# A one-core decoder layer: half-wise first unit, float32r conditioning sums, tiled forget gate, half-wise last scatter

## The chip, the cores and the metric

The kernel runs on one core of one Trainium2 chip. The metric is the device time of one launch, in microseconds. Before the change it was 780.5 us, the median of three runs (780.03 to 780.75).

## What is computed

One layer of a decoder trunk over x (1, 256, 1024), in float32, conditioned by one vector c (cut to what matters):

```python
mod = silu(c) @ W_ada + b_ada            # 6 x 1024: shift/scale/gate of the mixer and of the FFN
h = rms_norm(x) * (1 + scale_m) + shift_m
proj = h @ w_in                          # pool, sg_u, sg_v, conv_a, conv_g, q, k, v, f_logit (4), gates (4 x 1024)
y_a = multiscale_pool(z_pool);  y_b = spatial_gating(z_sg)
y_c = silu(layer_norm(causal_conv31(a * sigmoid(g))))
y_d = forgetting_attention(q, k, v, f_logit + b_f)   # softmax(qk + cum log_sigmoid(f))
merged = sum_n sigmoid(gates_n) * (y_n @ w_branch_n)
x = x + gate_m * (merged @ w_out)
h = rms_norm(x) * (1 + scale_f) + shift_f
x = x + gate_f * (moe(h) + shared(h))    # 64 experts, 6 per token, 1024 -> 256 -> 1024
return rms_norm(x)
```

## The kernel before, in words

Every engine's work stands in program order in one block per engine, and semaphores alone tie the blocks together. There is no planner: what an engine does next is what is written next.

**Weights.** SyncE (SP) streams all weights through a ring of 12 slots of 1 MB (L361: dense units in the order of `UNITS`; L364 and L369: experts). A load into a slot waits until the unit that was in it is used up. The last 16 `ada` units are used up by VectorE (`acc_done`), the others by TensorE. For the experts the ring holds two pairs; the loads of pair n+2 wait for TensorE's use of pair n (`w13_used`, `w2_used`).

**Start.** TensorE multiplies eight `ada` units with the conditioning vector (`ada(0)` to `ada(7)`, four column tiles of 32), and `columns(i)` turns the sums into columns. VectorE makes the scale a_c and shift s_c, and ScalarE (L478) and VectorE (L697) write the eight k-slices of hT, four after `columns(1)` and four after `columns(3)`, each counted by `h_done`.

**Mixer units.** `channels(i, u)` (L1166) runs 16 float32 products of 128x256; each is two MATMUL records. Units `mix 0` to `mix 7` are conv_g, conv_a, q, k, v, sg_v, sg_u and pool. All of them start after `h_done >= 8` (L1194). The forget logits are eight products with 4 columns of weights each, between units 2 and 3. VectorE adds the bias (L711) and, with ScalarE, makes log-sigmoid and its running sum; ScalarE then starts two small DMAs (L508, L509) that put the sums into the rows `qa[64]` and `ka[65]`, and the attention's logits on TensorE wait for them (`cum_rows`, L1206).

**Gate loop.** For g = 0 to 15 TensorE runs `channels(8 + g)` and then `branch(g - 3)` (LAG = 3) (L1275). At g = 3 it sums the convolution's channels, at g = 4 the squares (`cvar_done`). ScalarE takes one sigmoid per g (L557); at g = 4 it also does the layer norm's square root (L560) and the swish's sigmoid (L562). VectorE's order is: `conv_norm_1`, `accumulate(0)`, `conv_norm_2`, `accumulate(1)`, normalise and swish to `y[:, 2]` (L887 to L891), and then per g: `merge(g)`, at odd g from 3 on `cast_out`, `accumulate(g + 2)`. `accumulate(i)` adds four slices of a late `ada` unit, scaled, into `part2` (L753); two of them make one sum of 512 columns, and `cast(m)` on TensorE (L1250) adds that over the partitions by one float32 product with a matrix of ones, 128x512. Casts 0 to 5 run at g = 5, 7, ..., 15, `cast(6)` after the last branch.

**Out stage.** Four groups of eight 128x512 products with w_out, then `cast(7)` (L1324). VectorE does `accumulate(14)` and `accumulate(15)` before the first residual (`residual_2(0)`, L909).

**Experts.** Routing, then 32 pairs of experts; per pair the w1/w3 products, a gather for the next group, the scatter of the pair before, and the w2 products. VectorE splits each result into two float32r parts (L1076), counted by `y_split`; the scatter (L1392) waits for both halves. After the last pair the final scatter and norm follow.

Of the kernel before, what the change touches and what calls it, by code (L numbers as in the profile page):

```python
# [69 lines left out]
def unit_plan():  # L70
    units = [("ada", i) for i in range(8)] + [("mix", i) for i in range(8)]
    for g in range(N_GATE):
        if g % 4 == 3:
# [15 lines left out]
         "fold": 64, "inv": 512, "iota": CAP, "thr": 3, "mask": 384}  # L89
# [13 lines left out]
MISC = {"wf": KD * HEADS, "sg_w": HEADS * P, "pool_w": 2 * P, "sg_g": BW, "sg_beta": BW, "sg_bias": 2 * T}  # L103
# [7 lines left out]
def decoder_layer(nc, a, out):  # L111
    with ExitStack() as ctx:
# [50 lines left out]
        wf = mi("wf", "p (k h) -> p k h", h=HEADS)  # L163
# [26 lines left out]
        with ExitStack() as mixing:  # L190
            def early(name, shape):
                return mixing.enter_context(nc.sbuf_tensor(name, shape, F32))
# [24 lines left out]
            sig = c6(LAG + 2, 2 * T)  # L217
            gb = c6(2 * T)
            logit = sig[:, 0:2, 0:384]
            v_sb = sig[:, 2, :].rearrange("p (b c) -> p b c", b=TB)  # L220
# [9 lines left out]
            rden = early("rden", [P, HEADS, 2])  # L230
            fz = sig[0:HEADS, 3:5, :].rearrange("p a t -> p (a t)")[:, 0:3 * T].rearrange("p (r t) -> p r t", r=3)
# [16 lines left out]
        def gathered_row(parity, k):  # L248
# [21 lines left out]
        B_CAST = [3, 3, 3, 3, 3, 3, 3, 2]  # L270
# [15 lines left out]
            unit_done f_done f_read exp_f cum_done cum_rows  conv_done  # L286
# [4 lines left out]
            gb_done merged_done branch_done acc_done cast_done cast_read out_mm  # L291
# [3 lines left out]
            sw2_gated x2_top give_read y0_done y_gated y_top y_split pos_next sum_done x3_sq x3_var x3_rstd fin_done stored""".split()  # L295
# [162 lines left out]
        def _(act):  # L458
# [25 lines left out]
            def ub(i):  # L484
# [3 lines left out]
            act.activation(sig_c[:, :, :].rearrange("p j t -> p (j t)"), ub(0)[:, :], ACT.Sigmoid)\  # L488
               .then_inc(unit_read[0], 1)
            read_unit(2)  # L490
            act.wait_ge(S["zero_done"], 6)
# [59 lines left out]

            for g in range(N_GATE):

                read_unit(8 + g)
                if g >= LAG + 2:
                    act.wait_ge(S["gb_done"], g - LAG - 1)
                act.activation(sig[:, g % (LAG + 2), :], ub(g)[:, :], ACT.Sigmoid).then_inc(unit_read[g % 2], 1)  # L557
                if g == CONV_AT:
                    act.wait_ge(S["conv_var"], 1)
                    act.activation(mean_c[:, :], rs_c[:, :], ACT.Sqrt).then_inc(S["conv_rstd"], 1)  # L560
                    act.wait_ge(S["conv_n"], 2)
                    act.activation(sq_c[:, :, :], conv[:, :, :], ACT.Sigmoid).then_inc(S["conv_sig"], 1)  # L562
# [30 lines left out]

            square_2(0)
            square_2(1)
# [74 lines left out]
        def _(dve):  # L670
# [33 lines left out]
            dve.wait_ge(S["unit_done"], 2)  # L704
            dve.wait_ge(unit_read[0], 1)
# [5 lines left out]
            dve.tensor_scalar(fz[:, 0, :], bank[7][0:HEADS, 0:T], par[0:HEADS, P_AT["b_f"]:P_AT["b_f"] + 1], None,  # L711
# [155 lines left out]
            def cast_out(m):  # L867
# [3 lines left out]
                dve.wait_ge(S["cast_done"], m + 1)  # L871
# [7 lines left out]
                ins.then_inc(S["cast_read"], 1)  # L879

# [47 lines left out]
            residual_2(0)  # L928
            residual_2(1)
# [114 lines left out]
            def body(use):  # L1044
                for m in range(BODY_PAIRS):
# [21 lines left out]
                    for hf in range(2):  # L1067
                        if hf:
                            dve.wait_ge(w2_used[r], use * (BODY_PAIRS // 2) + m // 2 + 1)
                        else:  # L1070
# [6 lines left out]
                           .then_inc(S["y_split"], 1)  # L1077
# [38 lines left out]
        def _(pe):  # L1116
# [36 lines left out]
            ada(5)  # L1153
            ada(6)
            columns(2)
# [10 lines left out]
            def channels(i, u):  # L1166

                b, w = begin_unit(i, u)
                for m in range(2):
                    for k in range(KD):  # L1170
                        ins = mm(b[:, m * T:(m + 1) * T], w[:, k, m * P:(m + 1) * P], hT[:, k, :], k == 0, k == KD - 1)
                ins.then_inc(S["unit_done"], 1)
# [21 lines left out]
            pe.wait_ge(S["h_done"], 8)  # L1194
            channels(0, ("mix", 0))
# [79 lines left out]
            for g in range(N_GATE):  # L1275
# [13 lines left out]
                if g % 2 and g >= 5:  # L1289
                    cast((g - 5) // 2)  # L1290
# [4 lines left out]
            cast(6)  # L1295
# [28 lines left out]
            cast(7)  # L1324

# [75 lines left out]
            def body(use):  # L1401
                for m in range(BODY_PAIRS):
# [19 lines left out]
                    if not first:  # L1422
                        pe.wait_ge(S["y_split"], 2 * n)
# [9 lines left out]
                    if not first:  # L1433
                        scatter(1 - r, 0, opening)
                        scatter(1 - r, 1, opening)
# [43 lines left out]
            last = passes * (2 * PAIRS)  # L1479
            pe.wait_ge(S["give_read"], passes * PAIRS)  # L1480
            pe.wait_ge(S["y_split"], last)
            for hf in range(2):
                scatter(1, hf, stop=True).then_inc(S["sum_done"], 1)


def constants():
# [14 lines left out]
    c["iota"][:] = np.arange(CAP)  # L1501
    c["fold"][:] = i % E == np.arange(E)
# [4 lines left out]
def lay_out(inp):  # L1507
# [9 lines left out]
    wf = inp["w_in"][0][:, COL["f"]:COL["f"] + HEADS].reshape(KD, P, HEADS).transpose(1, 0, 2).reshape(P, KD * HEADS)  # L1517
# [35 lines left out]
```

## Time and profile before

| | |
|---|---|
| median of three runs | 780.5 us |
| the profiled execution | 781.12 us |
| its span, first to last instruction | 779.3 us |
| mean granted TensorE clock | 0.989 |
| PE busy | 730.0 us (94%) |
| PE weight loads | 387.9 us (50%) |
| DVE busy | 326.3 us (42%) |
| ACT busy | 172.2 us (22%) |
| HBM traffic | 271.33 MB, mean 348 GB/s |

PE is TensorE's matmuls, PEld its weight loads, DVE VectorE, ACT ScalarE, SPq the queue of SyncE. A busy share is an average over stages with different limits, so it doesn't say what a change in one stage is worth; the waits and the chain that ended last do.

### The profile page before, as it was taken

Reading aid. Unit: us, or ns where it says so; the run is one execution under the profiler, and the core shown is the slowest. Engines: PE = TensorE matmul, PEld = TensorE weight load, DVE = VectorE, ACT = ScalarE, POOL = GpSimd, SP = SyncE. Lnnn points to the kernel's source line nnn. Section 1 sums busy time; section 2 is a strip of 40 time slices with the busy share of each in tenths; the row PEclk is TensorE's granted clock in tenths of the full one; section 3 lists DMA queues with packets and bytes.
Section 4 is the critical chain, followed back from the end, with each engine's and each line's share of the span. In section 5 each row is a group of like instructions: output and inputs, shape, how many; then the busy total and the mean of one; then the engine's idle time right before and its main releaser. Section 6 shows DMA issues by size and latency. Waiting matters only on the chain.

```text
span 779.3 us, 12407 instructions
## 1 busy us (share of the span) xinstructions
PE 730.0 (94%) x5000; PEld 387.9 (50%) x5000; DVE 326.3 (42%) x814; ACT 172.2 (22%) x344; POOL 8.7 (1%) x22
## 2 busy tenths in 40 slices
PE   4799999999999999999999999999999999899894
PEld 1388888888887444334333343333334333333232
DVE  1107675674446577333334233231333333323325
ACT  3213240200000241222222122121222222212213
POOL 0200001000000000000000000000000000000000
PEclk9799999999999999999999999999999999999998
DMA  9999535777869676999999999999999999999981
GB/s 339 378 349 365 190 108 189 237 260 259 264 221 385 262 274 240 392 422 421 421 417 420 419 420 421 421 421 408 409 420 422 420 419 422 421 421 420 421 353 55
DMA packets 73571, 271.33 MB, mean 348 GB/s; under 512 B 4440, under 2 KB 33248, under 8 KB 48688
## 3 DMA queue, kind: packets, MB, share of 16 engines
q1 hardware_dynamic: 71808, 264.26, 86.3%
q0 software_dynamic: 1408, 6.20, 2.1%
q8 instruction: 40, 0.66, 0.3%
q10 hardware_dynamic: 304, 0.13, 0.1%
q14 instruction: 11, 0.09, 0.0%
HBM read 269.51 MB, written 1.05 MB: 347 GB/s over the span
## 4 chain that ended last, share of the span: by engine, by line
PE 67%; DMA 21%; DVE 6%; SPq 3%; ACT 2%; issue 1%; DVEq 0%; ACTq 0%
PE bank L1118 65%; DMA ring<-exp_w_dram 19%; DMA ring<-ada_w_dram 2%; SPq L364 1%; DVE slot_gate L1054 1%; SPq L361 1%; PE bank L1438 1%; DVE reg L1058 1%; DVE reg L1049 1%; ACT reg L632 1%; DMA reg<-reg 1%; DVE h_hT L1109 0%; PE bank L1138 0%; DVE stats L1096 0%; DVE bank L1072 0%
## 5 line engine op out<-in xcount | busy, mean ns | idle before, releaser
L1118 PE MATMUL bank<-ring,h_hT 128*32 128x512 f32 (+2 forms) x2112 | 255.4, 586 | 14.3 <-DMA ring<-exp_w_dram 13.5
L1118 PEld LDWEIGHTS bank<-ring,h_hT 128*32 128x32 f32 (+1 forms) x2112 | 84.6, 113 | 170.8 <-issue 151.2
L1118 PE MATMUL bank<-h_hT,ring 128*128 128x256 f32 x704 | 158.4, 385 | 1.8 <-ACT h_hT L478 1.8
L1118 PEld LDWEIGHTS bank<-h_hT,ring 128*128 128x128 f32 x704 | 135.5, 193 | 21.4 <-ACT h_hT L478 2.0
L1118 PE MATMUL bank<-ring,const_misc 128*32 128x512 f32 x1008 | 116.5, 595 | 0.3
L1049 DVE TENSOR_TENSOR reg<-reg,bank 128x256 f32<-128x256 f32 x32 | 13.5, 421 | 180.7 <-ACT reg L632 180.7
L1072 DVE TENSOR_TENSOR bank<-bank,reg 128x512 f32<-128x512 f32 x64 | 44.5, 695 | 54.6 <-PE bank L1118 54.6
L1076 DVE TENSOR_TENSOR y_part<-bank,y_part 128x512 fp32r<-128x512 f32 x64 | 44.3, 692 | 42.4 <-ACT y_part L645 21.2
L1118 PEld LDWEIGHTS bank<-ring,const_misc 128*32 128x32 f32 x1008 | 30.2, 109 | 61.6 <-issue 57.3
L632 ACT ACTIVATE reg<-bank 128x256 f32<-128x256 f32 x32 | 12.3, 384 | 198.8 <-PE bank L1118 198.8
L1118 PE MATMUL bank<-take,h_part 128*128 128x256 f32 x288 | 50.6, 299 | 0.4 <-ACT h_hT L617 0.2
L753 DVE SCALAR_TENSOR_TENSOR part<-ring,cact,part 128x512 f32<-128x512 f32 x56 | 42.0, 749 | 1.9 <-DVE part L753 0.2
L1118 PE MATMUL bank<-y_part,give 64*128 64x512 f32 x256 | 38.5, 418 | 2.4 <-DVE y_part L1076 2.4
L1118 PEld LDWEIGHTS bank<-take,h_part 128*128 128x128 f32 x288 | 38.8, 190 | 1.9 <-ACT h_hT L617 1.0
L627 ACT ACTIVATE h_hT<-bank 128x512 f32<-128x512 f32 x64 | 38.1, 595 | 3.8 <-PE bank L1118 0.3
L557 ACT ACTIVATE reg<-bank 128x512 f32<-128x512 f32 x16 | 9.6, 597 | 113.9 <-PE bank L1118 112.5
L643 ACT ACTIVATE y_part<-bank 128x512 fp32r<-128x512 f32 x32 | 19.1, 597 | 66.8 <-DVE bank L1072 66.8
L1118 PE MATMUL bank<-reg,ring 128*128 128x256 f32 x128 | 29.7, 379 | 0.0
L645 ACT ACTIVATE y_part<-bank 128x512 fp32r<-128x512 f32 x32 | 19.1, 597 | 43.6 <-DVE bank L1072 43.6
L862 DVE TENSOR_TENSOR reg<-bank,reg 128x512 f32<-128x512 f32 x16 | 11.1, 691 | 40.8 <-PE bank L1118 39.9
L1118 PE MATMUL bank<-ring,reg 128*128 128x512 f32 x64 | 27.8, 592 | 0.0
L1118 PEld LDWEIGHTS bank<-reg,ring 128*128 128x128 f32 x128 | 24.3, 190 | 5.9 <-issue 2.8
(231 smaller groups left out, 450.5 us busy)
## 6 DMA issues: line engine op xcount, KB each, us to landing
ring<-exp_w_dram SPq DMA_DIRECT2D x189, 1024.0 KB, 14.9
ring<-ada_w_dram SPq DMA_DIRECT2D x24, 1024.0 KB, 12.5
ring<-w_in_dram SPq DMA_DIRECT2D x24, 1024.0 KB, 12.3
ring<-w_branch_dram SPq DMA_DIRECT2D x4, 1024.0 KB, 12.9
ring<-w_out_dram SPq DMA_DIRECT2D x4, 1024.0 KB, 8.0
ring<-shared_w_dram SPq DMA_DIRECT2D x2, 1024.0 KB, 13.8
spare<-exp_w_dram SPq DMA_DIRECT2D x2, 1024.0 KB, 16.2
reg<-ada_bp_dram POOLq DMA_DIRECT2D x3, 512.0 KB, 8.3
```

What stands on the lines that cost most here:

```text
L361: sp.dma_start(dst, src).then_inc(landed[SLOT[u]], 16)
L557: act.activation(sig[:, g % (LAG + 2), :], ub(g)[:, :], ACT.Sigmoid).then_inc(unit_read[g % 2], 1)
L627: act.activation(gathered_row(1 - m // GROUP, 2 * (m % GROUP) + q), bank[B_GATH][:, :].rearrange("p (m s) -> p m s", m=GROUP), ACT.Copy)\
L632: act.activation(sg1[:, :], bank[B_HID][:, 0:FF], ACT.Sigmoid).then_inc(S["sig1_done"], 1)
L643: act.activation(y_part[0][:, 0:512], bank[B_Y[0]][:, :], ACT.Copy).then_inc(S["y_top"], 1)
L645: act.activation(y_part[0][:, 512:D], bank[B_Y[1]][:, :], ACT.Copy).then_inc(S["y_top"], 1)
L753: ins = dve.scalar_tensor_tensor(out=acc, in0=w[:, q, :], scalar=at, in1=acc, op0=ALU.mult, op1=ALU.add)
L862: dve.tensor_tensor(o, bank[4 + g % 2][:, :], sig[:, g % (LAG + 2), :], ALU.mult).then_inc(S["gb_done"], 1)
L1049: dve.tensor_tensor(th[:, :], sg1[:, :], bank[B_HID][:, 0:FF], ALU.mult).then_inc(S["th_done"], 1)
L1072: dve.tensor_tensor(bank[B_Y[hf]][:, :], bank[B_Y[hf]][:, :], gate_f[:, hf * 512:(hf + 1) * 512], ALU.mult)\
L1076: dve.tensor_tensor(y_part[1][:, cols], bank[B_Y[hf]][:, :], y_part[0][:, cols], ALU.subtract)\
L1118: return pe.matmul(o, lhsT, rhs, start=start, stop=stop, skip_group_check=True)
```

## The change

- The first mixer unit runs in two halves of k: its two outputs go to two banks (0 and 4), the first half of each after `h_done >= 4`, the second after `h_done >= 8`. `columns(2)` is moved ahead of `ada(6)`.
- The forget logits are computed in four column tiles of 32 (weights padded from 4 to 32 columns), copied out by ScalarE, and folded by one more product in the middle of unit 3.
- Each conditioning sum is cast in halves of 256 columns. ScalarE copies the half as float32r (`cast_top`), VectorE makes the rest (`cast_rest`), and TensorE adds two float32r products. There are 16 such casts; cast c stands ahead of `branch(c + 1)` at g = c + 4 for c = 0 to 11, the next two among the last branches, the last two behind the first and the second group of the out stage.
- `y_split` becomes `y_low` and `y_high`, and each half of the scatter waits for its own.

```diff
@@ ScalarE
             read_unit(0)
-            act.activation(sig_c[:, :, :]..., ub(0)[:, :], ACT.Sigmoid).then_inc(unit_read[0], 1)
+            act.activation(sig_c[:, 0, :], bank[B_UNIT_0[0]][:, 0:T], ACT.Sigmoid).then_inc(S["g_top"], 1)
+            act.activation(sig_c[:, 1, :], bank[B_UNIT_0[1]][:, 0:T], ACT.Sigmoid).then_inc(unit_read[0], 1)
             read_unit(2)
+            act.wait_ge(S["f_half"], 1)
+            act.activation(f_tiles[:, :], bank[7][:, 0:T], ACT.Copy).then_inc(S["f_tiled"], 1)
...
+            def cast_top(c):
+                act.wait_ge(S["acc_done"], 2 * (c // 2) + 2)
+                if c:
+                    act.wait_ge(S["cast_done"], c)
+                act.activation(cast_part[:, 0, :], part2[:, c // 2 % 2, (c % 2) * 256:(c % 2 + 1) * 256], ACT.Copy)\
+                   .then_inc(S["cast_top"], 1)
             for g in range(N_GATE):
...
+                if g >= LAG:
+                    cast_top(g - LAG)
...
+            cast_top(N_GATE - 3)
+            cast_top(N_GATE - 2)
             square_2(0)
+            cast_top(N_GATE - 1)
             square_2(1)
@@ VectorE
+            link(dve.tensor_copy(ones_r[:, :], cn("ones", 0, P)))
...
                 if half == 0 and m >= 2:
-                    dve.wait_ge(S["cast_done"], m - 1)
+                    dve.wait_ge(S["cast_rest"], 2 * (m - 1))
...
+            def cast_rest(c):
+                dve.wait_ge(S["cast_top"], c + 1)
+                dve.tensor_tensor(cast_part[:, 1, :], part2[:, c // 2 % 2, ...], cast_part[:, 0, :],
+                                  ALU.subtract).then_inc(S["cast_rest"], 1)
...
             for g in range(N_GATE):
                 merge(g)
+                if g not in (N_GATE - 3, N_GATE - 1):
+                    cast_rest(min(g, N_GATE - 3))
                 if g % 2 and g >= 3:
                     cast_out((g - 3) // 2)
                 if g + AHEAD < N_GATE - 2:
                     accumulate(g + AHEAD)
             accumulate(N_GATE - 2)
             accumulate(N_GATE - 1)
+            cast_rest(N_GATE - 2)
...
             residual_2(0)
+            cast_rest(N_GATE - 1)
             residual_2(1)
@@ TensorE
             ada(5)
+            columns(2)
             ada(6)
-            columns(2)
             ada(7)
             columns(3)
...
-            pe.wait_ge(S["h_done"], 8)
-            channels(0, ("mix", 0))
+            pe.wait_ge(S["h_done"], KD // 2)
+            w = begin_unit(0, ("mix", 0))[1]
+            for half in range(2):
+                if half:
+                    pe.wait_ge(S["h_done"], KD)
+                for m in range(2):
+                    for k in range(half * (KD // 2), (half + 1) * (KD // 2)):
+                        ins = mm(bank[B_UNIT_0[m]][:, 0:T], w[:, k, m * P:(m + 1) * P], hT[:, k, :], k == 0, k == KD - 1)
...
             for k in range(KD):
-                ins = mm(bank[7][0:HEADS, 0:T], wf[:, k, :], hT[:, k, :], k == 0, k == KD - 1)
-            ins.then_inc(S["f_done"], 1)
-            channels(3, ("mix", 3))
+                ins = mm(bank[7][32 * (k % 4):32 * (k % 4) + 32, 0:T], wf[:, k, :], hT[:, k, :], k < 4, k >= 4)
+            ins.then_inc(S["f_half"], 1)
+            channels(3, ("mix", 3), forget_sum)
...
-            def cast(m):
-                pe.wait_ge(S["acc_done"], 2 * m + 2)
-                if m:
-                    pe.wait_ge(S["cast_read"], min(m, 6))
-                mm(bank[B_CAST[m]][:, :], cn("ones", 0, P), part2[:, m % 2, :]).then_inc(S["cast_done"], 1)
+            def cast(c):
+                m, half = c // 2, c % 2
+                pe.wait_ge(S["cast_rest"], c + 1)
+                if m >= 2 and not half:
+                    pe.wait_ge(S["cast_read"], m - 1)
+                for i in range(2):
+                    ins = mm(bank[B_CAST[m]][:, half * 256:(half + 1) * 256], ones_r[:, :], cast_part[:, i, :], i == 0, i == 1)
+                ins.then_inc(S["cast_done"], 1)
...
-                if g % 2 and g >= 5:
-                    cast((g - 5) // 2)
+                if g > LAG:
+                    cast(g - LAG - 1)
                 if g >= LAG:
                     branch(g - LAG)
             for g in range(N_GATE - LAG, N_GATE):
                 branch(g)
-            cast(6)
+                if g != N_GATE - 2:
+                    cast([N_GATE - 4, None, N_GATE - 3][g - (N_GATE - LAG)])
...
-            cast(7)
+                if k < 2:
+                    cast(N_GATE - 2 + k)
...
-            pe.wait_ge(S["y_split"], last)
             for hf in range(2):
+                pe.wait_ge(S["y_high" if hf else "y_low"], last)
                 scatter(1, hf, stop=True).then_inc(S["sum_done"], 1)
```

`forget_sum` waits for `f_tiled` and runs one product `mm(bank[7][0:HEADS, T:2 * T], cn("fold_f"), f_tiles)`, which counts `f_done`; `channels` calls it between its two outputs.

## Rows read from the trace of the kernel before

**Rows 1.** Page, part 2: GB/s in 40 slices of the span.
```profile
GB/s 339 378 349 365 190 108 189 237 260 259 264 221 385 262 274 240 392 422 421 421 417 420 419 420 421 421 421 408 409 420 422 420 419 422 421 421 420 421 353 55
```
**Rows 2.** Chain that ended last: start us, us, what.
```profile
99.24 170.53 PE bank L1118 x754
...
463.91 19.16 DMA ring<-exp_w_dram
```
**Rows 3.** Timeline of SP's queue: start us, us, engine line, operation.
```profile
311.42 2.04 SPq L364 DMA_DIRECT2D ring<-exp_w_dram  x4
```
**Rows 4.** Timeline, start to first unit; in brackets idle before and its releaser.
```profile
28.14 0.20 PEld L1118 LDWEIGHTS bank<-ring,crep 128*32 128x32 f32 x8 [0.33 <-DMA ring<-ada_w_dram]
...
32.42 24.00 PE L1118 MATMUL bank<-h_hT,ring 128*128 128x256 f32 x96 [1.77 <-ACT h_hT L478]
```
**Rows 5.** First unit's load: issue (timeline), then its size and us to landing.
```profile
14.45 4.63 SPq L361 DMA_DIRECT2D ring<-w_in_dram  x1
...
ring<-w_in_dram SPq DMA_DIRECT2D x1, 1024.0 KB, 16.5
```
**Rows 6.** Windows: PE, PEld, DVE, ACT, POOL busy (x), PEclk, DMA share, GB/s.
```profile
25.00:28.00 3.00, 2.77 (x12) 0.92 (x12) 0.00 (x0) 0.00 (x0) 0.00 (x0) 0.50 1.06 377
...
33.00:38.00 5.00, 5.00 (x13) 4.01 (x12) 0.00 (x0) 0.66 (x1) 1.61 (x2) 0.50 1.06 396
```
**Rows 7.** Timeline of the forget logits, table load and rows; chain's line of their DMA.
```profile
56.34 3.62 PE L1118 MATMUL bank<-h_hT,const_misc 128*4 128x256 f32 x16
61.39 1.28 ACT L500 ACT_TABLE_LOAD   x1
62.68 0.41 ACT L500 ACTIVATE reg<-reg 4x256 f32<-4x256 f32 x1
64.29 0.28 DVE L722 TENSOR_SCALAR reg<-reg 4x256 f32<-4x256 f32 x1
...
68.36 5.84 DMA reg<-reg
...
74.34 2.86 PE L1118 MATMUL bank<-reg 66*128 66x128 f32 x16 [0.37 <-DMA reg<-reg]
```
**Rows 8.** Timeline: one cast, the out stage behind it; a gather and a scatter.
```profile
248.15 1.02 PE L1118 MATMUL bank<-part,const_misc 128*128 128x512 f32 x2
...
249.01 20.76 PE L1118 MATMUL bank<-ring,reg 128*128 128x512 f32 x48
...
324.95 0.68 PE L1118 MATMUL bank<-take,h_part 128*128 128x256 f32 x4
325.56 1.21 PE L1118 MATMUL bank<-y_part,give 64*128 64x512 f32 x8
```
**Rows 9.** Timeline around g = 4 of the gate loop, all engines.
```profile
140.46 0.60 ACT L557 ACTIVATE reg<-bank 128x512 f32<-128x512 f32 x1 [8.90 <-PE bank L1118]
...
141.13 1.89 PE L1118 MATMUL bank<-reg,ring 128*128 128x256 f32 x8
...
143.46 3.02 DVE L753 SCALAR_TENSOR_TENSOR part<-ring,cact,part 128x512 f32<-128x512 f32 x4
143.57 0.42 ACT L560 ACTIVATE reg<-reg 128x256 f32<-128x256 f32 x1 [1.21 <-DVE reg L851]
...
148.32 0.63 ACT L562 ACTIVATE reg<-reg 128x512 f32<-128x512 f32 x1 [3.03 <-DVE reg L888]
...
149.59 0.69 DVE L862 TENSOR_TENSOR reg<-bank,reg 128x512 f32<-128x512 f32 x1
```
**Rows 10.** Page, part 5: work on 256 columns; busy, mean ns, idle before.
```profile
L1049 DVE TENSOR_TENSOR reg<-reg,bank 128x256 f32<-128x256 f32 x32 | 13.5, 421 | 180.7 <-ACT reg L632 180.7
...
L632 ACT ACTIVATE reg<-bank 128x256 f32<-128x256 f32 x32 | 12.3, 384 | 198.8 <-PE bank L1118 198.8
```
**Rows 11.** Timeline: VectorE at the end of `accumulate(15)`, and in the tail.
```profile
253.43 3.12 DVE L753 SCALAR_TENSOR_TENSOR part<-ring,cact,part 128x512 f32<-128x512 f32 x4 [0.23 <-DVE part L753]
...
771.46 1.43 DVE L1096 BATCH_NORM_STATS2 stats<-bank 128x6 f32<-128x512 f32 x2 [0.90 <-PE bank L1118]
```

More of the change, by code:

```diff
@@ L88 @@
 CONST = {"ident": 128, "upper": 128, "strict": 128, "ones": 256,
-         "fold": 64, "inv": 512, "iota": CAP, "thr": 3, "mask": 384}
+         "fold": 64, "fold_f": HEADS, "inv": 512, "iota": CAP, "thr": 3, "mask": 384}
 C_AT, C_W = {}, 0
@@ L101 @@
     P_W += _w
-MISC = {"wf": KD * HEADS, "sg_w": HEADS * P, "pool_w": 2 * P, "sg_g": BW, "sg_beta": BW, "sg_bias": 2 * T}
+MISC = {"wf": KD * 32, "sg_w": HEADS * P, "pool_w": 2 * P, "sg_g": BW, "sg_beta": BW, "sg_bias": 2 * T}
 M_AT, M_W = {}, 0
@@ L161, in mi @@
             return misc[:, M_AT[name]:M_AT[name] + MISC[name]].rearrange(pattern, **kw)
-        wf = mi("wf", "p (k h) -> p k h", h=HEADS)
+        wf = mi("wf", "p (k h) -> p k h", h=32)
         sgw = mi("sg_w", "p (h t) -> p h t", h=HEADS)
@@ L190, in decoder_layer, with early @@
         with ExitStack() as mixing:
-            def early(name, shape):
-                return mixing.enter_context(nc.sbuf_tensor(name, shape, F32))
+            def early(name, shape, dt=F32):
+                return mixing.enter_context(nc.sbuf_tensor(name, shape, dt))
             reg1 = early("reg1", [P, 2 * D])
@@ L219, in decoder_layer @@
             logit = sig[:, 0:2, 0:384]
+            f_tiles = sig[:, 0, 0:T]
             v_sb = sig[:, 2, :].rearrange("p (b c) -> p b c", b=TB)
@@ L230, in decoder_layer @@
             rden = early("rden", [P, HEADS, 2])
+            ones_r = early("ones_r", [P, P], F32R)
+            cast_part = early("cast_part", [P, 2, 256], F32R)
             fz = sig[0:HEADS, 3:5, :].rearrange("p a t -> p (a t)")[:, 0:3 * T].rearrange("p (r t) -> p r t", r=3)
@@ L269, in decoder_layer @@
         B_UNIT = [0, 1]
-        B_CAST = [3, 3, 3, 3, 3, 3, 3, 2]
+        B_UNIT_0 = [0, 4]
+        B_CAST = [3, 2, 3, 2, 3, 2, 3, 2]
         B_OUT = [0, 1, 2, 3]
@@ L285, in decoder_layer @@
             final_in c_sig c_rep x_sq x_var x_rstd xn_done xT_done ada_done ada_read col_done acc_step ac_done h_done
-            unit_done f_done f_read exp_f cum_done cum_rows  conv_done
+            unit_done g_top f_half f_tiled f_done f_read exp_f cum_done cum_rows  conv_done
             q_done k_done tv_done sigv_done v_var v_rstd vn_done tu_done sigu_done
@@ L290, in decoder_layer @@
             logits_done logit_done exp_done prob_done pT_done pT_read av_done av_y
-            gb_done merged_done branch_done acc_done cast_done cast_read out_mm
+            gb_done merged_done branch_done acc_done cast_top cast_rest cast_done cast_read out_mm
             x2_done x2_sq x2_var x2_rstd h2_done h2T_done h2T_read
@@ L294, in decoder_layer @@
             take_built pair_gates gate_mm slot_gated gathered gath_read first_read sig1_done th_done hid_done turn_done turn_read
-            sw2_gated x2_top give_read y0_done y_gated y_top y_split pos_next sum_done x3_sq x3_var x3_rstd fin_done stored""".split()
+            sw2_gated x2_top give_read y0_done y_gated y_top y_low y_high pos_next sum_done x3_sq x3_var x3_rstd fin_done stored""".split()
         S = {n: sem(n) for n in names}
@@ L702, in _ @@
                 dve.tensor_tensor(sgw[:, h, :], sgw[:, h, :], cn("upper"), ALU.mult).then_inc(S["sgw_done"], 1)
+            link(dve.tensor_copy(ones_r[:, :], cn("ones", 0, P)))
             dve.wait_ge(S["unit_done"], 2)
+            dve.wait_ge(S["g_top"], 1)
             dve.wait_ge(unit_read[0], 1)
@@ L710, in _ @@
             dve.wait_ge(S["f_done"], 1)
-            dve.tensor_scalar(fz[:, 0, :], bank[7][0:HEADS, 0:T], par[0:HEADS, P_AT["b_f"]:P_AT["b_f"] + 1], None,
+            dve.tensor_scalar(fz[:, 0, :], bank[7][0:HEADS, T:2 * T], par[0:HEADS, P_AT["b_f"]:P_AT["b_f"] + 1], None,
                               ALU.add).then_inc(S["f_read"], 1)
@@ L870, in cast_out @@
                 dst = [gate_m, scale_b, shift_f, gate_f][m // 2][:, cols]
-                dve.wait_ge(S["cast_done"], m + 1)
+                dve.wait_ge(S["cast_done"], 2 * m + 2)
                 if m == 0:
@@ L879, in cast_out @@
                 ins.then_inc(S["cast_read"], 1)
+            def cast_rest(c):
+                dve.wait_ge(S["cast_top"], c + 1)
+                dve.tensor_tensor(cast_part[:, 1, :], part2[:, c // 2 % 2, (c % 2) * 256:(c % 2 + 1) * 256], cast_part[:, 0, :],
+                                  ALU.subtract).then_inc(S["cast_rest"], 1)
             conv_norm_1()
@@ L1076, in body @@
                         dve.tensor_tensor(y_part[1][:, cols], bank[B_Y[hf]][:, :], y_part[0][:, cols], ALU.subtract)\
-                           .then_inc(S["y_split"], 1)
+                           .then_inc(S["y_high" if hf else "y_low"], 1)
             with dve.Fori(0, 1) as use:
@@ L1164, in begin_unit, with forget_sum, channels @@
                 return bank[B_UNIT[i % 2]], unit(u).rearrange("p (k n) -> p k n", k=KD)
-            def channels(i, u):
+            def forget_sum():
+                pe.wait_ge(S["f_tiled"], 1)
+                mm(bank[7][0:HEADS, T:2 * T], cn("fold_f"), f_tiles[:, :]).then_inc(S["f_done"], 1)
+            def channels(i, u, between=None):
                 b, w = begin_unit(i, u)
                 for m in range(2):
+                    if m and between:
+                        between()
                     for k in range(KD):
@@ L1192, in turn_probs @@
                 ins.then_inc(S["pT_done"], 1)
-            pe.wait_ge(S["h_done"], 8)
-            channels(0, ("mix", 0))
+            pe.wait_ge(S["h_done"], KD // 2)
[6 more added lines that the diff above has]
+                        ins = mm(bank[B_UNIT_0[m]][:, 0:T], w[:, k, m * P:(m + 1) * P], hT[:, k, :], k == 0, k == KD - 1)
+            ins.then_inc(S["unit_done"], 1)
             channels(1, ("mix", 1))
@@ L1422, in body @@
                     if not first:
-                        pe.wait_ge(S["y_split"], 2 * n)
+                        pe.wait_ge(S["y_low"], n)
                     pe.wait_ge(S["pair_gates"], n + 1)
@@ L1434, in body @@
                         scatter(1 - r, 0, opening)
+                        pe.wait_ge(S["y_high"], n)
                         scatter(1 - r, 1, opening)
@@ L1478, in _ @@
                 body(use)
-            last = passes * (2 * PAIRS)
-            pe.wait_ge(S["give_read"], passes * PAIRS)
-            pe.wait_ge(S["y_split"], last)
+            last = passes * PAIRS
+            pe.wait_ge(S["give_read"], last)
             for hf in range(2):
+                pe.wait_ge(S["y_high" if hf else "y_low"], last)
                 scatter(1, hf, stop=True).then_inc(S["sum_done"], 1)
@@ L1501, in constants @@
     c["iota"][:] = np.arange(CAP)
+    c["fold_f"][:] = i % 32 == np.arange(HEADS)
     c["fold"][:] = i % E == np.arange(E)
@@ L1516, in lay_out @@
     par = np.concatenate(cols + [b_f], 1)
-    wf = inp["w_in"][0][:, COL["f"]:COL["f"] + HEADS].reshape(KD, P, HEADS).transpose(1, 0, 2).reshape(P, KD * HEADS)
+    wf = inp["w_in"][0][:, COL["f"]:COL["f"] + HEADS].reshape(KD, P, HEADS).transpose(1, 0, 2)
+    wf = np.pad(wf, ((0, 0), (0, 0), (0, 32 - HEADS))).reshape(P, KD * 32)
     sg_w = inp["sg_w"][0].transpose(2, 0, 1).reshape(P, HEADS * P)
```

2 lines of the change are left out of this document (removed).

## The prediction, made before the changed kernel ran

> **What bounds the kernel now.** I read the page's slices first. From about 312 us to 755 us the DMA moves some 420 GB/s in almost every slice [rows 1], so the experts go at the pace of their weights. Before that it moves 108 to 392 GB/s and something else is the limit. The chain of waits says what: from 99.24 to 269.77 us it is nothing but TensorE, and late in the expert stage it runs over the expert loads [rows 2]. Last I looked at the queue that issues the loads, to see what starts the saturated stream. Pair 2 of the experts is issued at 311.42 us [rows 3], as soon as TensorE has used pair 0's w1 and w3. From there the stream is full, so what is left after 311.42 us is bytes by 420 GB/s and a tail. Every microsecond that TensorE gains or loses before 311 us therefore shifts the end by the same amount; the sum below is one of TensorE's path up to there, and of the tail.
>
> **First unit in halves.** The four early slices of hT are ready before TensorE gets there (it still has `ada` units and `columns(3)` to do, written ahead of the unit). Now it waits 1.77 us for the last four slices and starts at 32.42 us [rows 4]. After the change it can start when `columns(3)` is out, at 30.65 us (32.42 - 1.77), unless the unit's weights are late: issued at 14.45 us, 16.5 us to land [rows 5], so 30.95 us. The start is 1.47 us earlier. Moving `columns(2)` ahead of `ada(6)` buys nothing: `ada(7)` already waits for its load [rows 4], and what was behind it now fills an idle gap. To the start comes the clock. It was granted at half (1.2 of 2.4 GHz) both from 25 to 28 us and from 33 to 38 us [rows 6]; in the second the first units lost 2.9 us: their 96 records took 24.0 us, where six times the 3.5 us of sixteen such records [rows 7] is 21.1. With less idle time in front of it I take a low stretch as short as the first one, which loses some 1.6 us instead of 2.9: another 1.3. Term: **-2.8**; with no low stretch -4.4, and if the earlier start is worth only half because the clock is low as long as before, -0.8.
>
> **Forget gate.** Sixteen records take 3.62 us, 3.55 us of TensorE's time [rows 7]. In four column tiles they should take a quarter, 0.9 us plus about 0.15 for filling, and the fold one 128x256 float32 product, 0.44 us. TensorE saves 2.1 us. But the logits behind wait for the two rows that the small DMA writes: they landed 0.37 us after TensorE was ready [rows 7]. That DMA needs unit 3 (now earlier by 2.1 us) and the running sum, which was ready 64.57 - 59.96 = 4.6 us after the logits. The logits now come 5.1 us after unit 2 (1.05, half of unit 3, the fold), the sum at 9.7, and the second DMA's issue near 10.4, with 5.84 us to landing [rows 7] 16.3 us, against 18.0 us now (56.34 to 74.34). Term: **-1.7** (-2.1 if the DMA is quicker, -1.2 if slower). ScalarE's extra copy (0.38 us) stands ahead of the q copies, which nobody waits for within 10 us; later VectorE work keeps 4 us or more of slack.
>
> **Casts as work.** A 128x512 float32 cast takes 0.86 us (248.15 to 249.01 [rows 8]). Four float32r products of 128x256 take 0.61 us until the next group starts (324.95 to 325.56 [rows 8]), 0.153 each, so a cast of 256 columns takes 0.31 us. Six casts leave the gate loop, thirteen come in up to the last branch: 13 x 0.31 - 6 x 0.86 = **-1.1**. The rows bound it from 0.2 us (the scatter's eight products, 1.21 us with their fill, handle twice the columns [rows 8]) to 0.5 us each: -2.6 to +1.3.
> The Trainium skill (TensorE: Matmul & The Clock Gate, Back-to-back issue gap) gives 262 cycles between products of 256 columns. By that rule a cast would take about 0.22 us, and the forecast would be 1.2 us lower; the gather in this trace is slower than that, and I go by the row.
>
> **The first cast as a wait.** This is the large term. Before, no cast stood at g = 4; now `cast(0)` does, in front of `branch(1)`, which started at 141.13 us [rows 9]. It waits for `cast_rest(0)`, and that stands on VectorE behind the whole layer norm of the convolution, which itself starts only from `cvar_done`, TensorE's instruction just before. And ScalarE now has `cast_top(0)` at g = 3, waiting for `accumulate(1)`; queued behind it are the sigmoid of g = 4 and the square root that the layer norm needs. In the times of before: `accumulate(1)` ends at 146.5 us (143.46 + 3.02 [rows 9]). Then ScalarE: copy 0.40 (384 ns [rows 10]), sigmoid 0.60, table load 1.30 (1.28 us, formerly hidden behind the wait for VectorE [rows 7, 9]), root 0.42 [rows 9]: 149.4. VectorE's four normalising steps took 1.7 us (146.6 to 148.32, where the swish started); now 151.1. Swish 0.63, product 0.61, so the first merge, 149.59 us before [rows 9], starts at 152.4, ends at 153.0, and `cast_rest(0)` (421 ns [rows 10]) at 153.4. TensorE stands still from 141.13 to 153.43: **+12.3** (11.8 to 12.8 by what the handovers add or save). Nothing hides it: `branch(1)` and the next unit, which filled that time, are now written behind the cast, and this engine runs its matmuls in the order in which they are written. Behind it the ring is full and VectorE catches up, since per unit it needs 0.42 (rest), 1.4 (merge), 0.7 to 1.4 (cast_out) and 3.1 us of TensorE's 9 (a unit's 7.1 and a branch's 1.9); so `cast(1)` and later ones should find their halves ready.
> The Trainium skill (ScalarE: Activation LUTs, What ACT_TABLE_LOAD costs) puts 1283 ns for the load and 1380 ns of drain on every switch of table. By that rule the exposed load would make the stall 1.4 us longer; in this trace an activation starts 0.01 us after a load ends (61.39 + 1.28 to 62.68 [rows 7]), so I count 1.30.
>
> **The clock after it.** TensorE has never idled for 12 us in the trace; after much shorter gaps in the first 40 us the clock was at half [rows 6]. So it should restart at 1.2 GHz. The two low stretches there cost 1.5 us (3 us at half) and 2.9 us: **+2.3** (1.5 to 3.1).
>
> **Out stage.** From the last branch (248.15 us): `cast(13)` 0.31, first group 20.76 / 3 = 6.9 us [rows 8], so TensorE reaches `cast(14)` at +7.2. VectorE first does both last accumulates, which ended at 256.55 us = +8.4 [rows 11]; then copy 0.40, rest 0.42 and handovers [rows 10]: +9.35. The stall is 2.15 us. `cast(14)` and `cast(15)` add 0.62, `cast(13)` 0.31, `cast(6)` leaves with 0.86; `cast(13)` is in the thirteen above, which leaves out the removed `cast(6)`, so the stage's own sum is 2.15 + 0.62 - 0.86 + 0.3 of rounding and fill: **+2.25** (1.5 to 2.9). The removed `cast(7)` gives nothing: VectorE's last residual ran beside it. After a 2.15 us gap the clock may fall too: 0 or 1.7 us, I take **+0.8**.
>
> **Tail.** The scatter of half 0 moves ahead, under the split of half 1. VectorE idled 0.90 us before two statistics steps of 1.43 us [rows 11]; the first now fills that gap: **-0.7** (0 to -0.9). Elsewhere in the expert stage the two waits change nothing, as weights are the limit.
>
> **Sum.** -2.8 - 1.7 - 1.1 + 12.3 + 2.3 + 2.25 + 0.8 - 0.7 = +11.4. The profiled execution took 781.1 us (span 779.3), so 792.5 for it; it is 0.6 us above the median of the runs, and the forecast for the median is 780.5 + 11.4 = **791.9 us**.
>
> **Rivals.**
> *Ready halves (other side, 5%).* The halves of `cast(0)` are made before TensorE gets there. Then +12.3 and +2.3 fall away: 777.3 us. The point that decides is whether `cast_rest(0)` ends before 141.13 us in the times of before. For it: the accumulates' data are there early. Against it: the first merge ran at 149.59 us [rows 9] and the rest is written behind it.
> *ScalarE not in the way (8%).* The root comes as early as before. The stall is then merge at 149.59 plus 1.05, 9.5 us: 789.1 us. Against it: the root is written behind `cast_top(0)`.
> *Hidden by the experts (4%).* The dense stage's loss is absorbed, because loads run ahead during the stall. Then only the tail moves: 779.8 us, no change. Against it: pair 2's load waits for TensorE [rows 3], and the ring holds two pairs only.
> *Every cast stalls (5%).* VectorE never catches up, and each of eleven later casts waits a microsecond: 803 us. Against it: the budget of about 6 of 9 us.
> The forecast has 78%.
>
> **Range and chances.** The terms' bounds added at their worst give 785 and 800 us; they are not all at one end, so 785.5 to 797 us, which takes in the second rival. About 0.2% (1.6 us) is what a measurement of this kernel can tell from no change. Faster 6%, same 4%, slower 90%.
>
> **What would show it.** An idle gap of some 12 us on TensorE before `cast(0)`, ended by VectorE's rest; ScalarE's sigmoid of g = 4 behind `accumulate(1)`; the granted clock at 0.5 just after; a gap near 2 us before `cast(14)`; unit 0 starting near 31 us; pair 2's load some 12 us later than 311.42, and the same 420 GB/s behind it. I am wrong if the gap is absent or the shift at pair 2 doesn't reach the end.

## The result

The changed kernel takes 791.1 us, the median of four runs (790.18 to 792.42), against 780.6 us for the kernel before (780.03 to 781.6): ratio 1.0133, 95% interval 1.0118 to 1.0148. It is 10.5 us slower. Its profiled execution took 792.4 us, with a span of 790.6 us against 779.3.

### The profile page after: what moved, and what is told of

It is laid out like the page before. It is cut to its first block, busy times and chain, and to the rows that moved or that the text cites. A ratio compares the mean times of both kernels' runs of the same rounds, so it can differ in the third digit from the quotient of the medians.

```text
span 790.6 us, 12494 instructions
## 1 busy us (share of the span) xinstructions
PE 725.0 (92%) x5018; PEld 387.5 (49%) x5018; DVE 331.8 (42%) x831; ACT 177.8 (22%) x362; POOL 8.7 (1%) x22
## 4 chain that ended last, share of the span: by engine, by line
PE 63%; DMA 21%; DVE 8%; SPq 3%; ACT 2%; issue 2%; DVEq 0%; ACTq 0%
PE bank L1150 62%; DMA ring<-exp_w_dram 18%; DMA ring<-w_in_dram 2%; SPq L365 2%; SPq L368 1%; DVE slot_gate L1086 1%; PE bank L1488 1%; DVE reg L1090 1%; DVE part L775 1%; DVE reg L1081 1%; ACT reg L652 1%; DMA reg<-reg 1%; DVE reg L884 0%; DVE h_hT L1141 0%; DVE reg L887 0%
## 5 line engine op out<-in xcount | busy, mean ns | idle before, releaser
L652 ACT ACTIVATE reg<-bank 128x256 f32<-128x256 f32 x32 | 12.3, 384 | 200.3 <-PE bank L1150 200.3
L571 ACT ACTIVATE reg<-bank 128x512 f32<-128x512 f32 x16 | 9.5, 596 | 108.3 <-PE bank L1150 108.3
L1150 PEld LDWEIGHTS bank<-y_part,give 64*128 64x128 f32 x256 | 21.6, 184 | 9.9 <-DVE y_part L1108 1.6
## 6 DMA issues: line engine op xcount, KB each, us to landing
ring<-ada_w_dram SPq DMA_DIRECT2D x24, 1024.0 KB, 12.8
ring<-w_branch_dram SPq DMA_DIRECT2D x4, 1024.0 KB, 12.8
```

The source lines that it names most:

```text
L652: act.activation(sg1[:, :], bank[B_HID][:, 0:FF], ACT.Sigmoid).then_inc(S["sig1_done"], 1)
L1150: return pe.matmul(o, lhsT, rhs, start=start, stop=stop, skip_group_check=True)
```

## The profile after

The page of the changed kernel first: total busy time and the slices. PE's busy time fell by 5 us and its share from 94% to 92%; the rate of the experts' stage is the same 420 GB/s, but it starts about half a slice later: slice 17 has 298 GB/s where it had 392 [rows 1].

```profile
span 790.6 us, 12494 instructions
PE 725.0 (92%) x5018; PEld 387.5 (49%) x5018; DVE 331.8 (42%) x831; ACT 177.8 (22%) x362; POOL 8.7 (1%) x22
GB/s 339 379 348 364 199 81 235 217 76 367 177 337 271 368 145 332 298 412 419 421 420 420 421 422 421 420 421 421 377 419 422 421 418 422 422 419 421 423 368 54
```

Next the chain that ended last, the rows that answer to the one long piece of TensorE [rows 2]; they are from the list of its longest pieces, so short ones between them are left out. It is now broken between 138 and 150 us and once more before 265.90:

```profile
96.05 42.07 PE bank L1150 x220
138.64 1.63 issue
144.30 1.28 ACT L574
150.07 102.31 PE bank L1150 x478
265.90 14.47 PE bank L1150 x36
```

The timeline of the changed kernel around g = 4, all engines, answers to [rows 9]. TensorE ends the sum of squares at 138 us and does nothing until VectorE's `cast_rest(0)` (L906) is out; cuts between the lines are marked. ScalarE's first float32r copy (L563) waited 15.00 us for `accumulate(1)`, and only behind it come the sigmoid of g = 4 (L571), the table load and the root (L574):

```profile
137.08 1.03 PE L1150 MATMUL bank<-reg,const_misc 128*128 128x256 f32 x4
...
140.27 3.02 DVE L775 SCALAR_TENSOR_TENSOR part<-ring,cact,part 128x512 f32<-128x512 f32 x4
...
143.38 0.42 ACT L563 ACTIVATE cast_part<-part 128x256 fp32r<-128x256 f32 x1 [15.00 <-DVEq L780]
143.70 0.58 ACT L571 ACTIVATE reg<-bank 128x512 f32<-128x512 f32 x1
...
144.30 1.28 ACT L574 ACT_TABLE_LOAD   x1
145.59 0.42 ACT L574 ACTIVATE reg<-reg 128x256 f32<-128x256 f32 x1
...
147.73 0.63 ACT L576 ACTIVATE reg<-reg 128x512 f32<-128x512 f32 x1 [0.42 <-DVE reg L916]
...
149.00 0.68 DVE L884 TENSOR_TENSOR reg<-bank,reg 128x512 f32<-128x512 f32 x1
149.60 0.41 DVE L906 TENSOR_TENSOR cast_part<-part,cast_part 128x256 fp32r<-128x256 f32 x1
...
150.07 0.80 PE L1150 MATMUL bank<-cast_part,ones_r 128*128 128x256 f32 x2 [11.96 <-DVE cast_part L906]
...
150.66 3.05 PE L1150 MATMUL bank<-reg,ring 128*128 128x256 f32 x8
```

L576 is the swish, which before ran at 148.32 us (L562). The same `branch(1)` took 1.89 us before and 3.05 us here. The windows of the changed kernel (busy per engine, granted clock third from the right) say why: the clock fell to half during the idle time and was back at full in the window from 153 us.

```profile
138.00:141.00 3.00, 0.11 (x1) 0.00 (x0) 2.79 (x4) 0.00 (x0) 0.00 (x0) 1.00 1.03 374
141.00:144.00 3.00, 0.00 (x0) 0.00 (x0) 2.22 (x3) 0.62 (x2) 0.00 (x0) 0.79 0.11 43
...
147.00:150.00 3.00, 0.00 (x0) 0.00 (x0) 2.27 (x6) 0.94 (x2) 0.00 (x0) 0.50 1.05 341
150.00:153.00 3.00, 2.93 (x8) 2.48 (x9) 2.67 (x5) 0.42 (x1) 0.00 (x0) 0.50 0.32 110
153.00:156.00 3.00, 3.00 (x15) 2.64 (x15) 1.79 (x4) 0.00 (x0) 0.00 (x0) 1.00 0.67 183
```

TensorE in the changed kernel at the places of [rows 4, 7, 8]: the first unit, the forget logits in tiles, their fold, the attention's logits, a cast in the loop with its branch, and the cast in the out stage that waits.

```profile
31.01 14.18 PE L1150 MATMUL bank<-h_hT,ring 128*128 128x256 f32 x51 [0.58 <-DMA ring<-w_in_dram]
...
54.83 1.07 PE L1150 MATMUL bank<-h_hT,const_misc 128*32 128x256 f32 x16
...
59.48 0.59 PE L1150 MATMUL bank<-reg,const_misc 128*4 128x256 f32 x2
...
71.16 2.86 PE L1150 MATMUL bank<-reg 66*128 66x128 f32 x16 [0.52 <-DMA reg<-reg]
...
160.27 0.59 PE L1150 MATMUL bank<-cast_part,ones_r 128*128 128x256 f32 x2
...
162.42 7.07 PE L1150 MATMUL bank<-h_hT,ring 128*128 128x256 f32 x32
169.14 0.58 PE L1150 MATMUL bank<-cast_part,ones_r 128*128 128x256 f32 x2
169.56 1.89 PE L1150 MATMUL bank<-reg,ring 128*128 128x256 f32 x8
171.29 7.07 PE L1150 MATMUL bank<-h_hT,ring 128*128 128x256 f32 x32
...
265.90 0.50 PE L1150 MATMUL bank<-cast_part,ones_r 128*128 128x256 f32 x2 [1.63 <-DVE cast_part L906]
```

Pair 2's load in the changed kernel, which answers to [rows 3]: 10.6 us later than 311.42.

```profile
322.03 2.25 SPq L368 DMA_DIRECT2D ring<-exp_w_dram  x4
```

The tail of the changed kernel: the scatter is split in two, and the first statistics step (L1128) has no wait in front any more [rows 11].

```profile
780.78 0.73 PE L1150 MATMUL bank<-y_part,give 64*128 64x512 f32 x4 [0.55 <-DVE y_part L1108]
...
782.51 0.69 DVE L1128 BATCH_NORM_STATS2 stats<-bank 128x6 f32<-128x512 f32 x1
...
782.65 0.73 PE L1150 MATMUL bank<-y_part,give 64*128 64x512 f32 x4 [1.14 <-DVE y_part L1108]
...
783.50 0.70 DVE L1128 BATCH_NORM_STATS2 stats<-bank 128x6 f32<-128x512 f32 x1 [0.29 <-PE bank L1150]
```

## The experiments

All times are medians, beside the kernel before on the same chip (780.96 us for e1 to e4, 780.77 us for e5 to e8, spread 777.7 to 782.8). The ratios are not the quotients of the medians: 775.99 to 780.96 is 0.9936 where the ratio of e3 is 0.9941, so a difference of medians can be half a microsecond or more off what the ratio says.

The traces allow a comparison that leaves the start of the kernel, and its clock, out: the distance from the attention's logits on TensorE to pair 2's load.

| | attention's logits | pair 2's load | distance, us |
|---|---|---|---|
| before | 74.34 | 311.42 | 237.08 |
| changed | 71.16 | 322.03 | 250.87 |
| e1_late_cast | 71.09 | 309.25 | 238.16 |
| e2_scalar_order | 71.00 | 320.27 | 249.27 |
| e3_old_casts | 68.71 | 305.79 | 237.08 |
| e4_unit_twice | 74.31 | 318.27 | 243.96 |
| e5_late_both | 68.27 | 304.42 | 236.15 |
| e6_products_twice | 70.88 | 310.33 | 239.45 |
| e7_no_halves | 71.31 | 308.40 | 237.09 |
| e8_old_casts_again | 68.19 | 305.27 | 237.08 |

**e1_late_cast.** Every cast of the gate loop one unit later, and behind the branch instead of ahead of it: `cast(0)` goes from before `branch(1)` to behind `branch(2)`. `cast(13)`, `cast(14)` and `cast(15)` stay where they were. ScalarE's `cast_top` and VectorE's `cast_rest` move along.

```diff
 # ScalarE                                   # VectorE
-if g >= LAG: cast_top(g - LAG)             -if g not in (13, 15): cast_rest(min(g, 13))
+if g > LAG: cast_top(g - LAG - 1)          +if g not in (1, 15): cast_rest(max(g - 1, 0))
 # TensorE
-if g > LAG: cast(g - LAG - 1)
 if g >= LAG: branch(g - LAG)
+if g > LAG + 1: cast(g - LAG - 2)
...
-if g != N_GATE - 2: cast([N_GATE - 4, None, N_GATE - 3][g - (N_GATE - LAG)])   # last three branches
+cast(g - 2)
```

> The changed kernel with its casts one unit later: cast(c) stands behind branch(c + 2) at g = c + 5, cast_top(c) one unit later on ScalarE, cast_rest(c) one merge later on VectorE (only rest 0 stays behind the first merge). Theory (the first cast's wait is the loss): the stall of 12.1 us before cast(0) goes, and with it 1.3 us at half clock; 10.6 us above before becomes about 2.8 below, 777.5 us. Rival (the casts as such cost TensorE or VectorE more than they save, wherever they stand): less than 6 us of the loss comes back, 785 us or more. Rival (the delay was not what reached the end): no change from 791 us.

Measured: 778.3 us (ratio to before 0.9962, 0.9946 to 0.9978). The kernel is 12.8 us faster than the change as written. TensorE of e1 at the same place: its only stop there is half a microsecond for the first merge, and `cast(0)` stands behind `branch(2)` without a wait.

```profile
137.88 1.89 PE L1151 MATMUL bank<-reg,ring 128*128 128x256 f32 x8
139.60 7.07 PE L1151 MATMUL bank<-h_hT,ring 128*128 128x256 f32 x32
147.17 1.97 PE L1151 MATMUL bank<-reg,ring 128*128 128x256 f32 x8 [0.50 <-DVE reg L885]
148.79 0.59 PE L1151 MATMUL bank<-cast_part,ones_r 128*128 128x256 f32 x2
```

What follows: the place of the casts was the loss, and the trace shows of which: the stop of 12 us before `cast(0)` went, the wait before `cast(14)` in the out stage stayed (1.77 us). The distance of the table is 12.7 us shorter than in the change. The same casts in other places make the change faster than before, by 0.2 to 0.5%. No run moved `cast(0)` alone on TensorE, or `cast_rest(0)` alone on VectorE.

**e2_scalar_order.** Only ScalarE's order: `cast_top(0)` stands behind the root and the swish of g = 4 (CONV_AT is 4).

```diff
+if g == CONV_AT: cast_top(0)      # behind root and swish
-if g >= LAG: cast_top(g - LAG)
+if g > LAG: cast_top(g - LAG)
```

> The changed kernel, with only ScalarE's cast_top(0) moved from g = 3 to behind the square root and the swish of g = 4; TensorE's and VectorE's order is unchanged. Theory (VectorE's order makes most of the stall, ScalarE's queue the rest): the gap before cast(0) shrinks from 12.1 to about 9.3 to 9.7 us, the time to about 788.5 us. Rival (ScalarE's queue is the whole cause): the gap falls below 3 us and the time to about 779. Rival (it adds nothing): 791 us.

Measured: 787.8 us (ratio 1.0097, 1.0081 to 1.0113). The gap before `cast(0)` in e2, here in the timeline with ScalarE's root back in its old place (it waits 1.21 us for VectorE as it did before):

```profile
147.32 0.80 PE L1152 MATMUL bank<-cast_part,ones_r 128*128 128x256 f32 x2 [9.37 <-DVE cast_part L908]
147.91 3.62 PE L1152 MATMUL bank<-reg,ring 128*128 128x256 f32 x8
151.32 7.57 PE L1152 MATMUL bank<-h_hT,ring 128*128 128x256 f32 x32
158.54 0.59 PE L1152 MATMUL bank<-cast_part,ones_r 128*128 128x256 f32 x2
```
```profile
140.23 0.42 ACT L574 ACTIVATE reg<-reg 128x256 f32<-128x256 f32 x1 [1.21 <-DVE reg L875]
```

So of 12 us, 2.6 were ScalarE's queue and 9.4 VectorE's order. Both single-cause readings fall: ScalarE is not the whole, and it is not nothing. The clock took part of it back: cast, branch and unit behind the wait take 11.22 us in e2 (147.32 to 158.54) and 10.20 us in the changed kernel (150.07 to 160.27, when `cast(1)` starts), where at the full clock they take 8.87. So the distance of the table shrank by 1.6 us and not by 2.6.

**e3_old_casts and e8_old_casts_again.** The change without its casts; the banks of the casts are those of before again too. e8 is the same kernel as e3, measured beside e5 to e7.

```diff
-float32r casts in halves (cast_top, cast_rest, 16 casts)
+mm(bank[B_CAST[m]][:, :], cn("ones", 0, P), part2[:, m % 2, :])   # 8 casts, places of before
```

> The changed kernel with the casts of before (eight float32 products of 128x512, their old places), so only the first unit in halves, the tiled forget gate and the half-wise last scatter are left of the change. Theory (terms measured in the two traces: -1.5, -1.7, -0.7): 3.9 us below before, 776.7 us, saturated expert loads issued 3.2 us earlier than 311.42. Rival (the experts' loads hide gains of the dense stage): only the tail's 0.7 us shows, 779.9 us.

> The same kernel as e3_old_casts, to stand beside e5 and e7 on one chip. Theory: 776 us; e5 (float32r casts placed without waits) equals it within 1 us, as 16 x 0.23 us of casts stand against 7 x 0.86 us on the path and ScalarE and VectorE carry the rest: e5 2 us below at best. The clock at the start may differ from e3's: with a low stretch 777 to 778, without 775.

Measured: 776.0 us (ratio 0.9941, 0.9928 to 0.9954) and 775.3 us (0.9945, 0.9924 to 0.9966), 5.0 and 5.5 us below before instead of 3.9. Pair 2's load was issued at 305.79 us, 5.6 us earlier than before. In e3 and e8 the clock was granted in full at the start, where before had a low stretch [rows 6]. In e3's trace that is worth 3.0 of the 5.6 us: the 96 records of the first units take 20.96 us against 24.00 [rows 4]. From the attention's logits on, before, e3 and e8 need the same 237.08 us. By the ratios the gain is 4.6 and 4.3 us, and 3.9 lies within both intervals. The window of e3, and of e1, where the clock was low as well:

```profile
33.00:38.00 5.00, 5.00 (x25) 4.40 (x24) 0.00 (x0) 0.83 (x1) 1.77 (x2) 1.00 1.06 392
```
```profile
33.00:38.00 5.00, 5.00 (x17) 4.15 (x16) 0.00 (x0) 1.00 (x1) 1.50 (x2) 0.67 1.05 395
```

**e4_unit_twice.** The kernel before, with one dense unit computed twice.

```diff
+if g == 5: the 16 products of channels(8 + g), once more, same bank and start flags
 channels(8 + g, ("gate", g))
```

> The kernel before, with gate unit g = 5 computed twice in place (16 more float32 products of 128x256, same result). Theory (TensorE's path up to pair 2's load passes one to one to the end): plus 6.9 us, 787.5 us, and pair 2's load issued 6.9 us later. Rival (the experts' loads absorb a delay of the dense stage): plus 0 to 2 us.

Measured: 787.5 us (ratio 1.0076, 1.0062 to 1.0091), plus 6.5. Pair 2's load in e4 is issued at 318.27 us, 6.85 later; nothing of it is absorbed by the experts' loads within what the runs can tell (the interval of the ratio is 4.8 to 7.1 us). This is the one-to-one passage on which the whole sum rests, shown by itself.

```profile
142.82 13.98 PE L1118 MATMUL bank<-h_hT,ring 128*128 128x256 f32 x64
```
```profile
318.27 2.06 SPq L364 DMA_DIRECT2D ring<-exp_w_dram  x4
```

**e5_late_both.** e1, and the out stage's casts one group later.

```diff
-if k < 2: cast(N_GATE - 2 + k)
+if k in (1, 2): cast(N_GATE - 3 + k)
 residual_2(0)
-cast_rest(N_GATE - 1)
 residual_2(1)
+cast_rest(N_GATE - 1)
```

> e1_late_cast, and in the out stage cast(14) behind the second group of products and cast(15) behind the third, with cast_rest(15) behind the second residual. Theory (the wait for the two last accumulates is the only loss of the out stage): the gap of 1.77 us before cast(14) in e1 goes, 776.5 us; pair 2's load issued 1.8 us before e1's 309.25 where the clock at the start is the same. Rival (moved casts delay the norm behind them, so another wait takes the place): as e1, 778.3 us.

Measured: 775.8 us (ratio 0.9942, 0.9924 to 0.9961), 2.6 below e1. Part of that is the clock, full at the start of this profile and low in e1's; without it, by the table, e5 is 2.0 us shorter than e1, for a gap of 1.77. The gap itself is gone in the trace: two groups run through, and the cast behind them has no wait.

```profile
241.45 13.95 PE L1151 MATMUL bank<-ring,reg 128*128 128x512 f32 x32
254.84 0.81 PE L1151 MATMUL bank<-cast_part,ones_r 128*128 128x256 f32 x2
```

Beside e8, whose clock was also full, pair 2's load comes at 304.42 against 305.27 us: rightly placed, the float32r casts are worth 0.85 us (0.93 by the table) of TensorE's path, less than the runs can tell (775.8 and 775.3 us). e3/e8 and e5 are the best versions, equal within the measurement.

**e6_products_twice.** e5 with each cast's two products done twice.

```diff
-for i in range(2):
+for i in (0, 1, 0, 1):
```

> e5 with both float32r products of each cast computed twice (same result, 32 more products of 128x256). Theory (a float32r product costs TensorE 0.11 to 0.12 us where other work stands around it, as the 0.23 us per cast in the trace of the changed kernel say): 16 casts x 0.22 = plus 3.5 us over e5. Rival (0.153 us each, as in the gather of the kernel before, which my prediction used): plus 4.9 us. Rival (casts are hidden): plus less than 1 us.

Measured: 778.9 us (ratio 0.9984, 0.9968 to 0.9999), 3.1 over e5, though e6's profile had a low clock at the start and e5's had not, so the times alone don't separate 3.5 from 4.9. The trace of e6 does, with the start of a cast and of the unit behind it: 0.67 us apart, against 0.43 in e1 (148.79 to 149.22), so 0.12 us for each product more. The whole agrees: by the table e6 needs 3.30 us more than e5, 0.10 us for each of the 32 products, so the rival of 4.9 us is out.

```profile
148.57 0.83 PE L1151 MATMUL bank<-cast_part,ones_r 128*128 128x256 f32 x4
149.24 7.07 PE L1151 MATMUL bank<-h_hT,ring 128*128 128x256 f32 x32
```

**e7_no_halves.** e3 with the first unit undivided and `columns(2)` behind `ada(6)` again.

```diff
-pe.wait_ge(S["h_done"], KD // 2)   # and the loop over halves
+pe.wait_ge(S["h_done"], 8)
+channels(0, ("mix", 0))
```

> e3_old_casts with the first unit undivided and columns(2) back behind ada(6): forget gate and last scatter alone. Theory: 2.4 us below before, 778.3 us; the first unit starts 1.4 us later than in e3, and what e3 gains beyond 3.9 us over before is the granted clock at the start (half from 31.7 to 38.5 us in before, full in e3). Then this kernel should show the low stretch again more often than not and lie about 2 us above e3. Rival (the halves are worth their earlier start only): 1.4 us above e3.

Measured: 777.7 us (ratio 0.9972, 0.9958 to 0.9986), 1.7 and 2.4 above e3 and e8. That doesn't separate the 2 us of the theory from the 1.4 us of the rival. The unit starts at 32.46 us against 31.0 in e8. Whether the halves bring a better clock can't be read from the profiles: with halves the profiles show a low stretch near 30 to 37 us in the changed kernel, e1, e2 and e6 and none in e3, e5 and e8; without halves there is one in before, e4 and e7, shorter in e7. Each is one execution, and both kinds occur with the same first 40 us of code. All executions together say more, as each has a mean granted clock: it was 0.994 or more in 23 of 40 executions of the kernels with halves (e1, e3, e5, e6, e8) and in 16 of 57 of those without (before, e4, e7). That speaks for the halves, but the mean doesn't tell where a low stretch lay, so it stays likely and not shown. Executions at a like clock are few, but they agree with the terms. With a mean of 0.994 or more, in the session of e5 to e8: median 778.9 us before (8), 776.6 in e7 (4), 775.3 in e8 (4). So the forget gate and the tail bring 2.3 us, with the halves 3.6, near the 2.4 and 3.9 of the terms.

## Why the prediction was right, term by term

The forecast was 791.9 us, measured 791.1; as a change of time, +11.4 and +10.5. The terms, read from the two profiled traces as shifts of one and the same work:

| term | forecast | measured | how read |
|---|---|---|---|
| first unit, start | -1.5 | -1.4 | 32.42 to 31.01 |
| first unit, clock | -1.3 | -0.1 | forget logits 56.34 to 54.83 |
| forget gate | -1.7 | -1.7 | attention's logits 74.34 to 71.16, less the above |
| stall before `cast(0)` | +12.3 | +12.1 | 141.13 - 3.18 to 150.07 |
| clock after it | +2.3 | +1.35 | `branch(1)` and `cast(0)` against their later likes |
| casts as work | -1.1 | -1.6 | from +10.7 at unit g = 5 to +8.7 behind the last branch, and `cast(0)`'s own 0.4 |
| out stage | +2.25 | +1.9 | to +10.6 at the last group, and at 322.03 |
| clock after it | +0.8 | 0 | granted 1.00 |
| experts' stream | 0 | +1.4 | pair 2's load to the last pair: 442.9 and 444.3 us |
| tail | -0.7 | -0.7 | last pair to the end: 24.97 and 24.23 |
| sum | +11.4 | +11.2 | span +11.3 |

*The mechanism held.* The chain of waits that the prediction wrote out came in its order and its size, to 0.2 us over 12. e1 and the traces show that the place of `cast(0)` is the cause; e2 splits it as the rival "ScalarE not in the way" priced it, 9.4 measured and 9.5 foreseen. "Ready halves" is out, as the wait was there. "Every cast stalls" is out too: in the changed kernel every later cast up to the last branch stood without a wait, but for 0.17 us before `cast(13)`, and in e1 all up to there did. "Hidden by the experts" is out by e4.

*What was luck.* That the sum comes out to 0.2 us is luck. The terms of TensorE's path and the tail were forecast as +11.4 and measured +9.85, 1.5 us less, and the experts' stream, forecast as nothing, was 1.4 us longer in this execution. The large terms don't owe anything to that.

*Terms mis-sized.* The clock at the start was expected to improve and did not in this execution; e3, e5 and e8 show that it can, worth up to 3 us, and that with the same code at the start it differs between executions. The clock after the stall cost 1.35 instead of 2.3 us, below the term's bounds of 1.5 to 3.1: the low stretch had begun during the idle time and ended 3 us after work began, the shorter of the two lengths that I had rows for. In e2, behind a wait of 9.37 us, it cost 2.35 us (11.22 against 8.87), so the term isn't a fixed one. `cast(14)`'s gap drew no low clock, at 1.6 us. And a cast in float32r costs 0.23 us of TensorE's time where I took 0.31 from the gather: a unit, cast and branch take 8.87 us (162.42 to 171.29) against 8.64 for a unit and a branch in the kernel before (152.34 to 160.98). The upper bound of 0.5 us that I gave this term came from no row. By the Trainium skill's figure (TensorE: Matmul & The Clock Gate, Back-to-back issue gap), which I had set aside, it would have been 0.22 as an estimate, and the trace agrees with it.
The Trainium skill's drain with each table switch (ScalarE: Activation LUTs, What ACT_TABLE_LOAD costs) would have put 1.4 us more into the stall. The trace does not: the sigmoid ends at 144.28, the load runs from 144.30 to 145.58 and the root starts at 145.59.

*The experts' stream* was 1.4 us longer in the profiled execution; in e1 to e8 it lay between 443.0 and 443.9 us. The profiled execution was also the slowest of the four. What made it longer, and what it was in the others, isn't known.

*What the change's parts are worth:* first unit, forget gate and tail together 5.0 to 5.5 us faster (e3, e8), of which the trace of the changed kernel accounts for 3.9 and the clock at the start for the rest, as far as it is more than the spread; the casts as written 13.8 us slower than the old ones by the table (250.87 against 237.08; the medians, 791.1 and 776.0, have differences of the stream and of the clock at the start in them), rightly placed nothing that can be measured.

## What to carry to other kernels

A cheaper operation on the bounding engine is worth nothing where it is written ahead of its inputs: before pricing it, list what stands on each other engine between the point where that engine is free and the operation's last input, and put the operation behind other ready work. A copy for one purpose in an in-order queue (here ScalarE's, which waited 15 us) also holds whatever is behind it, and the two delays add in one chain. And where a stage's end starts a saturated stream of loads, a microsecond of it is a microsecond of the whole; doubling one unit shows it in one run.

## What the runs showed of the hardware that I had not expected

- The same first 40 us of code ran at the full clock in some executions and at half for some 6 us in others (window 33 to 38 us: granted 0.67 in e1, 1.00 in e3). Pair 2's load came 4.8 us later in e1 (low) than in e5 (full), of which 2.0 come behind the attention's logits, with e1's gap before `cast(14)`. The other 2.8 us are there already at the logits (71.09 and 68.27), before any cast, and 2.5 of them are the clock's: the 96 records of the first units take 23.46 us in e1 and 20.96 in e5. That fits the spread of the kernel before: of its 26 executions beside e5 to e8, the 13 with a mean clock of 0.992 or less took 780.7 to 782.8 us, the 8 with 0.994 or more 777.7 to 779.7.
- A float32r product of 128x256 with the same weight matrix each time costs 0.10 to 0.12 us among float32 work (e6), while four of them in the gather took 0.153 each [rows 8]. A unit of float32 products in front of a float32r cast takes 6.72 us until the cast starts (162.42 to 169.14 in the changed kernel), and 6.91 in front of float32 work (152.34 to 159.25 in the one before).
- In the changed kernel TensorE was idle for 12 us, and the granted clock was 0.50 from 147 to 153 us, of which the last 3 us were work, and 1.00 behind it. The low clock cost 1.35 us there and 2.35 us in e2, behind an idle time of 9.37 us. Behind the 1.63 us before `cast(14)` it stayed at 1.00.
